# Second block of a fused two-block kernel: k_dil's projection before the first turns, a first quarter of w_out before the last turns, and the last columns by halves of the tokens

## The chip, the cores and the metric

One core of one Trainium2 chip runs the whole program. The metric is device time in microseconds (us) of one launch. Before: median 1310.07 us of three runs (1309.26 to 1310.48).

## The reference, cut to what matters

The first block (a mixer and an expert-choice mixture of 16 experts) is not touched. The second block works on x of 256 tokens x 1024 columns, all in fp32:

```python
h = rms_norm_2(x, mix_norm_g[i])
u = h @ w_in[i]                       # 1024 -> 4096
dq, dk, dv, bq, bk, bv, z = jnp.split(u, IN_SPLIT_IDX, axis=-1)
# dq, dk, bq, bk are normalised over heads of 64
a = diff_attention(dq, dk, dv, lam, diff_slopes)   # 4 heads, two softmaxes each
a = rms_norm_2(a, diff_sub_norm_g[i]) * (1.0 - lam_init)
b = dilated_attention(bq, bk, bv, dil_slopes)      # 8 heads
y = jnp.concatenate([a, b], axis=-1) * jax.nn.silu(z)
x = x + y @ w_out[i]
gate = jax.nn.sigmoid(rms_norm_2(x, ple_norm_g[i]) @ w_ple_gate[i])
x = x + gate * (p[i] @ w_ple_proj[i])
```

## The kernel before, in words

**Weights.** A large product is done as three fp32r matmuls: weights and activations are each split into a high part and a remainder (`split_product`). `split(name, i)` is the work for one 1 MB slot of weights: ScalarE copies it to fp32r (the high part, L1458), then VectorE subtracts (the low part, L1849); TensorE waits for the latter. There are three places for high parts, so ScalarE can start a slot's copy only when TensorE has done the third slot before it.

**Units.** TensorE works through `TAIL_UNITS` in order. A unit is a projection (`q_diff`, `k_diff`, `q_dil`, `k_dil`, `v_diff`, `v_dil`: `rows_product`, 48 matmuls of 512 columns; `z0`, `z1`: 96 of 256) or a set of 8 transposes of 128x128 (the `turn_` units) or a product of weights of the attention with v (`pv_`). Unit u writes banks 0 and 1 of PSUM if u is even, 2 and 3 if odd, so it needs those that unit u-2 filled to have been read (`begin`, semaphores `tfree`). Of most units ScalarE reads the first bank and VectorE the second; both banks of q_diff, k_diff, q_dil and k_dil are read by ScalarE alone (a Square and a Copy each, L1675 and L1676).

**Scores.** After the units in `SCORES_AFTER`, `score_product(a)` (L1300, 16 matmuls) fills banks 4 to 7: a = 0, 1 are the two halves of the queries of the differential attention, 2, 3 those of the dilated. It waits for the reads of turn_q and turn_k. VectorE then does `score_rows(a)` (L2262, four ops) and `score_max(a)` (L2267), ScalarE `exponentials(a)` (L1655, eight ops), VectorE for a = 0, 1 `diff_weights(a)` (L2273 to L2279), and `turn_w0` and `turn_w1` transpose what comes out. `qk_sums` (L2230, L2232), `head_root` (ScalarE, L1661) and `qk_rows` (L2239, L2243) normalise the heads of one projection; a turn_q or turn_k unit waits for its qk_rows.

**Order.** Each engine's order of work is written out by hand, with waits on semaphores between engines. Nothing overtakes on VectorE or ScalarE: a unit's read stands in the written order. In the kernel before, on VectorE, score_rows(1) and score_max(1) follow qk_rows(2), and qk_sums(3), diff_weights(0), v_diff's read, qk_rows(3), diff_weights(1), v_dil's read and turn_w0's come behind them; ScalarE has exponentials(1) directly behind the split of v_dil's second slot, ahead of v_diff's read and both splits of z0.

**End.** `out_product(0..3)` multiplies with quarters of w_out into banks 4 to 7, once `cat_rest` has given the gated activations (`yt_ready`). `add_half(n)` (L2366) adds columns half n to x, `turn_quarter` (L883) transposes it by quarters, `split_pair` makes high parts (ScalarE, L1463) and low ones (VectorE, L1859), and four `columns_rows` products with w_gate follow.

Of the kernel before, what the change touches and what calls it, by code (L numbers as in the profile page):

```python
# [24 lines left out]
P = 128  # L25
SEQ, D = 256, 1024
TT = SEQ // P
KD = D // P
# [32 lines left out]
def shape_constants():  # L61
# [11 lines left out]
    for window, dilation in ((128, 1), (512, 4), (2048, 16)):  # L73
# [16 lines left out]

OPENING = ("fourier_in", "v0", "c0")
STEPS, STEP_K = 4, 2
TAIL_UNITS = [("q_diff", 2), ("k_diff", 2), ("q_dil", 2), ("turn_k_diff", 0), ("turn_q_diff", 0), ("scale_row", 0), ("k_dil", 2),
              ("v_diff", 2), ("v_dil", 2), ("turn_w0", 0), ("turn_k_dil", 0), ("turn_q_dil", 0), ("turn_w1", 0), ("pv_diff", 0),
              ("z0", 2), ("turn_e0a", 0), ("turn_e0b", 0), ("pv_dil0", 0), ("z1", 2), ("turn_e1a", 0), ("turn_e1b", 0),
              ("turn_cat0", 0), ("pv_dil1", 0), ("turn_cat1", 0)]

SCORES_AFTER = {"scale_row": 0, "k_dil": 1, "turn_w1": 2, "turn_e0b": 3}

ROWS_UNITS = ("fourier_in", "q_diff", "k_diff", "v_diff", "q_dil", "k_dil", "v_dil")  # L100

# [16 lines left out]
def build(nc, t, out):  # L118
    ctx = ExitStack()
    with ctx:  # L120
# [613 lines left out]
        def _(pe):  # L734
# [115 lines left out]
                        before_last(last)  # L850
                last.then_inc(slot_used, 1)

            def rows_product(s, u, await_pair=None):

                for i in range(2):
                    w = split_slot(s + i, k=FG, n=BANK)
                    for pair in range(2) if await_pair else (None,):
                        if await_pair:
                            await_pair(2 * i + pair)
                        for tt in range(TT):  # L860
                            for kk in (2 * pair, 2 * pair + 1) if await_pair else range(FG):
                                k = FG * i + kk
                                last = split_product(bank(2 * (u % 2) + tt), [a[:, k, tt * P:(tt + 1) * P] for a in (ht_hi, ht_lo)],
                                                     [h[:, kk, :] for h in w], k == 0, k == KD - 1)
                            if k == KD - 1 and tt == 0:
                                end_first(last)
                        if await_pair and i and pair == 0:
                            turn_stream_back()
                    last.then_inc(slot_used, 1)

            def begin(sems, u):

                for j in range(2):
                    if reads_before(sems, u):
                        pe.wait_ge(sems[pair_of(sems, u) + j], reads_before(sems, u))

            def turn_quarter(rows, q, b):

                for c in range(2):
                    for tt in range(TT):  # L880
                        to = bank(b, c=2, t=TT, m=P)[:, c, tt, :]
                        cols = slice((2 * q + c) * P, (2 * q + c + 1) * P)
                        last = nc.tensor.transpose(to, rows[:, tt, cols], ident)  # L883
                last.then_inc(norm_turned, 1)

            def sum_partitions(b):
# [417 lines left out]
            def out_product(i):  # L1304

                pe.wait_ge(yt_ready, i + 1)
                w = split_slot(first_slot["w_out"] + i, k=2, n=D)
                for n in range(2):
                    for kk in range(2):
                        k = 2 * i + kk  # L1310
                        for tt in range(TT):
                            last = split_product(bank(4 + 2 * tt + n), [a[:, k, tt * P:(tt + 1) * P] for a in (ht_hi, ht_lo)],
                                                 [h[:, kk, n * BANK:(n + 1) * BANK] for h in w], k == 0, k == KD - 1)
                    if i == 3 and n == 0:
                        last.then_inc(out_half, 1)
                last.then_inc(slot_used, 1)

            for u, (name, slots) in enumerate(TAIL_UNITS):
                begin(tfree, u)
                if name == "scale_row":  # L1320
                    pe.wait_ge(xr_ready, 4)
                    for tt in range(TT):
# [2 lines left out]
                elif name in ("z0", "z1"):  # L1325
                    transposed_product(first_slot[name], u, (ht_hi, ht_lo))
                elif name in IN2_CHUNK:
                    rows_product(first_slot[name], u, await_entry if u == 0 else None)
                elif name.startswith(("turn_q", "turn_k")):
                    i = ("turn_q_diff", "turn_k_diff", "turn_q_dil", "turn_k_dil").index(name)  # L1330
                    pe.wait_ge(qn_ready, 2 * i + 2)
                    for j in range(2):
                        for c in range(2):
                            for tt in range(TT):
                                last = nc.tensor.transpose(bank(2 * (u % 2) + j, c=2, t=TT, m=P)[:, c, tt, :],  # L1335
                                                           qn[i][:, tt, (2 * j + c) * P:(2 * j + c + 1) * P], ident)
                        end_first(last) if j == 0 else end_second(last, 0)
                elif name.startswith("turn_w"):

                    a = int(name[6])  # L1340
                    pe.wait_ge(w_ready, a + 1)
                    for j in range(2):
                        for c in range(2):
                            for kk in range(TT):
                                last = nc.tensor.transpose(bank(2 * (u % 2) + j, c=2, t=TT, m=P)[:, c, kk, :],
                                                           scores[a][:, 2 * (2 * j + c), kk * P:(kk + 1) * P], ident)
                        end_first(last) if j == 0 else end_second(last, 0)
                elif name.startswith("turn_e"):
                    a, part = int(name[6]), "ab".index(name[7])
                    pe.wait_ge(exps_done, 3 + a)  # L1350
                    for j in range(2):
                        for c in range(2):
                            for kk in range(TT):
                                last = nc.tensor.transpose(bank(2 * (u % 2) + j, c=2, t=TT, m=P)[:, c, kk, :],
                                                           scores[a][:, 4 * part + 2 * j + c, kk * P:(kk + 1) * P], ident)
                        end_first(last) if j == 0 else end_second(last, 0)
# [19 lines left out]
                else:  # L1376
# [3 lines left out]
                    else:  # L1380
                        await_read(pe, tfree, tail_u["pv_dil0"])
                        await_read(pe, tfree, tail_u["pv_dil1"])
                    for j in range(2):
                        for c in range(2):
                            for tt in range(TT):
                                last = nc.tensor.transpose(bank(2 * (u % 2) + j, c=2, t=TT, m=P)[:, c, tt, :],
                                                           cat[:, tt, (4 * i + 2 * j + c) * P:(4 * i + 2 * j + c + 1) * P], ident)
                        end_first(last) if j == 0 else end_second(last, 0)
                if name in SCORES_AFTER:
                    score_product(SCORES_AFTER[name])  # L1390
            pe.wait_ge(scores_read, 16)
            for i in range(4):
                out_product(i)
            await_read(pe, tfree, len(TAIL_UNITS) - 2)
            await_read(pe, tfree, len(TAIL_UNITS) - 1)
            def await_half(q):

                if q % 2 == 0:
                    pe.wait_ge(x_ready, X_MIXED + 6 + q)

            for q in range(4):
                await_half(q)
                turn_quarter(x, q, q)
            pe.wait_ge(x_ready, X_MIXED + 8)
            for c in range(4):
                columns_rows(first_slot["w_gate"] + c, lambda tt: bank(gate_bank(c, tt))[:, 0:HALF], (ht_hi, ht_lo),
# [5 lines left out]
        def _(act):  # L1412
# [331 lines left out]
            split("k_dil", 0)  # L1744
            split("k_dil", 1)
            unit("q_dil")
            unit("turn_k_diff")
            unit("turn_q_diff")
            split("v_diff", 0)
            unit("scale_row")  # L1750
            head_root(2)
            split("v_diff", 1)
            exponentials(0)
            split("v_dil", 0)
            unit("k_dil")
            split("v_dil", 1)
            exponentials(1)
            head_root(3)
            unit("v_diff")
            split("z0", 0)  # L1760
            split("z0", 1)
            unit("v_dil")
            unit("turn_w0")
# [45 lines left out]
        def _(dve):  # L1809
# [552 lines left out]
            def add_half(n):  # L2362

                cols = slice(n * BANK, (n + 1) * BANK)
                for tt in range(TT):
                    V.tensor_tensor(x[:, tt, cols], x[:, tt, cols], bank(4 + 2 * tt + n), ALU.add).then_inc(x_ready, 1)  # L2366

            split_entry(0)
# [30 lines left out]
            split("k_dil", 0)  # L2399
            split("k_dil", 1)  # L2400
            scale_x()
            unit("turn_k_diff")
            qk_sums(2)
            unit("turn_q_diff")
            score_rows(0)
            split("v_diff", 0)
            unit("scale_row")
            score_max(0)
            split("v_diff", 1)
            qk_rows(2)  # L2410
            split("v_dil", 0)
            score_rows(1)
            score_max(1)
            split("v_dil", 1)
            qk_sums(3)
            lambda_sums()
            diff_weights(0)
            unit("v_diff")
            qk_rows(3)
            diff_weights(1)  # L2420
            unit("v_dil")
            unit("turn_w0")
# [23 lines left out]
            unit("turn_e1a")  # L2446
            unit("turn_e1b")
            cat_gate(0)
            split("w_out", 1)
            dil_rows(1)  # L2450
            cat_rest(0, 0)
            cat_rest(0, 1)
            z_gate(1)
            cat_gate(1)
# [2 lines left out]
            split("w_out", 3)  # L2457
            cat_rest(1, 1)
            split("w_gate", 0)
            dve.wait_ge(out_half, 1)  # L2460
            add_half(0)
            dve.wait_ge(slot_used, first_slot["w_out"] + 4)
            add_half(1)
            for q in range(4):
                split_pair(q, q, col[:, C_PLE:C_PLE + KD], 4)
# [52 lines left out]
```

## Time and profile before

| What | Value |
|---|---|
| median of three runs | 1310.07 us |
| profiled execution: its time, its span | 1309.2 us, 1307.4 us |
| TensorE busy, over the span | 978.1 us (75%) |
| VectorE, ScalarE busy | 385.5 us (29%), 247.1 us (19%) |
| mean granted TensorE clock, share of full speed | 0.882 |
| projections of the second block begin | 1130.99 us |
| last VectorE op ends | 1305.14 us |

Times in views are from the start of the span. In a timeline a row is start, duration, engine, line, operation, operands and count; the brackets behind it give how long the engine had been idle and what ended that. A row's duration includes a tail of some 0.1 us in which the engine's next instruction may already start, so the pitch between the starts of neighbouring rows is what work costs in a queue. In the chain of work that ended last, matmuls stand without this overlap.

### The profile page before, as it was taken

The page shows a single profiled execution, that of the slowest core. Times are in us where ns is not written, and L with a number is a line of the kernel's source. Part 1 is how long each engine was busy: PE and PEld are TensorE (multiplying, and loading weights), DVE is VectorE, ACT ScalarE, POOL GpSimd, SP SyncE. Part 2 cuts the span into 40 slices and gives each one's busy share as a digit, 9 for nine tenths or more (in the row PEclk, how much of TensorE's full clock was granted, in tenths as well). Part 3 has the DMA queues.
Part 4 walks back from the last instruction along what each step waited for, and adds up shares of the span by engine and source line. Part 5 has one row for each costly group of instructions (what it writes and reads, how often), then busy time and mean ns, then how long its engine had stood idle before and what let it go on. Part 6 is the DMA issues. An engine that isn't in the chain of part 4 may idle for free.

```text
span 1307.4 us, 15592 instructions
## 1 busy us (share of the span) xinstructions
PE 978.1 (75%) x6744; PEld 559.2 (43%) x6744; DVE 385.5 (29%) x590; ACT 247.1 (19%) x376; POOL 21.3 (2%) x47
## 2 busy tenths in 40 slices
PE   9999999968565665646666656666665675899998
PEld 7899998323121221212122121212121221478988
DVE  5888866200010110000011000001010000488865
ACT  4454434000000000000000000000000000467744
POOL 2000200000000000000000000000000000000000
PEclk9999999999778878788778787879788878999999
DMA  9998999999999999999999999999999999965230
GB/s 337 389 386 326 314 384 420 401 429 431 426 430 433 432 431 432 425 432 437 428 430 431 429 430 438 431 428 430 431 430 435 431 433 418 397 226 164 95 129 33
DMA packets 70204, 496.43 MB, mean 380 GB/s; under 512 B 4842, under 2 KB 27002, under 8 KB 49680
## 3 DMA queue, kind: packets, MB, share of 16 engines
q1 hardware_dynamic: 67840, 489.11, 90.6%
q0 software_dynamic: 2080, 6.55, 1.6%
q8 instruction: 35, 0.57, 0.2%
q10 hardware_dynamic: 240, 0.11, 0.0%
q14 instruction: 9, 0.07, 0.0%
HBM read 494.71 MB, written 1.06 MB: 379 GB/s over the span
## 4 chain that ended last, share of the span: by engine, by line
DMA 56%; PE 39%; SPq 2%; DVE 1%; issue 1%; ACT 0%; DVEq 0%
DMA ring<-in_w_down_e 23%; DMA ring<-in_w_up_e 18%; DMA ring<-in_w_gate_e 15%; PE psum L748 8%; PE psum L750 8%; PE psum L749 8%; PE psum L1217 7%; PE psum L1247 4%; SPq L571 1%; PE psum L1258 1%; SPq L584 1%; DMA ring<-in_w_in 1%; PE psum L1300 1%; PE psum L1194 1%; PE psum L1335 0%
## 5 line engine op out<-in xcount | busy, mean ns | idle before, releaser
L1217 PE MATMUL psum<-ring,arena 128*32 128x512 f32 x2048 | 300.4, 734 | 186.1 <-DMA ring<-in_w_up_e 109.8
L1247 PE MATMUL psum<-ring,arena 128*32 128x512 f32 x976 | 158.8, 777 | 104.6 <-DMA ring<-in_w_down_e 103.9
L1217 PEld LDWEIGHTS psum<-ring,arena 128*32 128x32 f32 x2048 | 69.4, 129 | 377.5 <-issue 168.5
L1247 PEld LDWEIGHTS psum<-ring,arena 128*32 128x32 f32 x976 | 41.5, 132 | 205.2 <-issue 136.9
L1849 DVE TENSOR_TENSOR ring_r<-ring,ring_r 128x2048 fp32r<-128x2048 f32 x49 | 111.1, 2288 | 35.8 <-ACT ring_r L1458 35.6
L1626 ACT ACTIVATE arena<-psum 128x512 f32<-128x512 f32 x16 | 9.6, 598 | 532.1 <-PE psum L1217 532.1
L748 PE MATMUL psum<-ht_hi,ring_r 128*128 128x256 f32 x384 | 108.5, 283 | 0.0
L750 PE MATMUL psum<-ht_hi,ring_r 128*128 128x256 f32 x384 | 107.3, 279 | 0.0
L749 PE MATMUL psum<-ht_lo,ring_r 128*128 128x256 f32 x384 | 107.2, 279 | 0.0
L2211 DVE TENSOR_TENSOR arena<-psum,arena 128x512 f32<-128x512 f32 x32 | 20.6, 686 | 291.8 <-PE psum L1247 291.8
L1458 ACT ACTIVATE ring_r<-ring 128x2048 fp32r<-128x2048 f32 x49 | 92.5, 1910 | 29.7 <-PE psum L750 22.6
L2204 DVE TENSOR_TENSOR arena<-psum,arena 128x512 f32<-128x512 f32 x16 | 11.1, 692 | 266.9 <-ACT arena L1626 266.9
L748 PE MATMUL psum<-ring_r,ht_hi 128*128 128x256 f32 (+1 forms) x256 | 87.0, 340 | 0.2 <-issue 0.2
L750 PE MATMUL psum<-ring_r,ht_lo 128*128 128x256 f32 (+1 forms) x256 | 86.9, 339 | 0.0
L749 PE MATMUL psum<-ring_r,ht_hi 128*128 128x256 f32 (+1 forms) x256 | 86.1, 336 | 0.0
L1258 PE MATMUL psum<-arena 128*128 128x256 f32 x256 | 65.8, 415 | 13.5 <-DVE arena L2211 13.5
L748 PEld LDWEIGHTS psum<-ht_hi,ring_r 128*128 128x128 f32 x384 | 72.1, 188 | 1.6 <-issue 1.4
L749 PEld LDWEIGHTS psum<-ht_lo,ring_r 128*128 128x128 f32 x384 | 72.2, 188 | 0.2
L750 PEld LDWEIGHTS psum<-ht_hi,ring_r 128*128 128x128 f32 x384 | 72.1, 188 | 0.0
L1258 PEld LDWEIGHTS psum<-arena 128*128 128x128 f32 x256 | 51.8, 208 | 39.7 <-DVE arena L2211 32.1
L1630 ACT ACTIVATE arena<-psum 128x512 f32<-128x512 f32 x16 | 9.6, 597 | 294.6 <-PE psum L1235 294.6
L748 PEld LDWEIGHTS psum<-ring_r,ht_hi 128*128 128x128 f32 x256 | 48.1, 188 | 6.3 <-issue 1.1
(307 smaller groups left out, 934.1 us busy)
## 6 DMA issues: line engine op xcount, KB each, us to landing
ring<-in_w_gate_e SPq DMA_DIRECT2D x23, 4096.0 KB, 33.3
ring<-in_w_up_e SPq DMA_DIRECT2D x22, 4096.0 KB, 33.3
ring<-in_w_down_e SPq DMA_DIRECT2D x21, 4096.0 KB, 33.9
ring<-in_w_up_e SPq DMA_DIRECT2D x16, 2048.0 KB, 36.3
ring<-in_w_in SPq DMA_DIRECT2D x31, 1024.0 KB, 9.9
ring<-in_w_gate_e SPq DMA_DIRECT2D x14, 2048.0 KB, 36.5
ring<-in_w_down_e SPq DMA_DIRECT2D x14, 2048.0 KB, 36.9
ring<-in_w_ada SPq DMA_DIRECT2D x16, 1024.0 KB, 9.8
```

The source lines that it names most:

```text
L571: sp.dma_start(slot_in(s, k=FG, part=2, n=STEP_K * P)[:, :, part, :], head_stream[s][:, :, part, :]).then_inc(loaded[place(s)], 16)
L584: sp.dma_start(slot_in(s, k=FG, n=BANK)[:, rows, :], head_stream[s][:, rows, :]).then_inc(opening_loaded[name], 16)
L748: mm(to, left[0], right[0], start=start, stop=False)
L749: mm(to, left[0], right[1], start=False, stop=False)
L750: return mm(to, left[1], right[0], start=False, stop=stop)
L1194: last = mm(bank(tt), pt[k][:, tt * P:(tt + 1) * P], w_pp[:, k, n * BANK:(n + 1) * BANK], start=(k == 0), stop=(k == 1))
L1217: last = mm(psum[32 * g:32 * g + 32, b, :].rearrange("s (q c) -> s q c", c=4), cur[h][:, k, :], w[:, g // 2, :, g % 2 * 4:g % 2 * 4 + 4], ...
L1247: last = mm(psum[32 * q:32 * q + 32, 2 + n, :], act_t[:, f % 4, (f // 4) * CAP:(f // 4 + 1) * CAP], w[:, kk, n * BANK:(n + 1) * BANK], sta ...
L1258: last = mm(bank(4 + q, c=2, s=SEQ)[:, c, :], y[:, n, at:at + P], gwt.rearrange("p t m -> p (t m)"), start=False, stop=True, skip_group_ch ...
L1458: f(ring_r[part_place[s]][:], ring[:, place(s), :], ACT.Copy).then_inc(hi_ready, 1)
L1849: V.tensor_tensor(ring_r[place(s)][:], ring[:, place(s), :], ring_r[part_place[s]][:].bitcast(F32), ALU.subtract).then_inc(lo_ready, 1)
L2211: V.tensor_tensor(y[:, n, :], bank(2 + n), gf_row[:, n * BANK:(n + 1) * BANK], ALU.mult).then_inc(y_ready, 1)
```

## The change

TensorE: unit k_dil moves ahead of turn_k_diff, turn_q_diff and scale_row (which changes the pair of banks of these four), and the second scores follow v_diff and not k_dil. The wait for the second bank of a projection or a turn stands behind the work into the first bank. out_product(0) is done between pv_dil1 and turn_cat1. In the last w_out quarter the second half of the columns is done token half by token half, and the addition and the turns behind it follow by token halves. VectorE and ScalarE get new orders in the first part; VectorE does cat_rest(0, 0) before the split of w_out's second quarter. The slots of weights are loaded in the same order as before. The core of the diff (the second-bank wait is added in the same way in the other turn branches):

```diff
-TAIL_UNITS = [("q_diff", 2), ("k_diff", 2), ("q_dil", 2), ("turn_k_diff", 0), ("turn_q_diff", 0), ("scale_row", 0), ("k_dil", 2),
+TAIL_UNITS = [("q_diff", 2), ("k_diff", 2), ("q_dil", 2), ("k_dil", 2), ("turn_k_diff", 0), ("turn_q_diff", 0), ("scale_row", 0),
               ("v_diff", 2), ("v_dil", 2), ("turn_w0", 0), ("turn_k_dil", 0), ("turn_q_dil", 0), ("turn_w1", 0), ("pv_diff", 0),
...
-SCORES_AFTER = {"scale_row": 0, "k_dil": 1, "turn_w1": 2, "turn_e0b": 3}
+SCORES_AFTER = {"scale_row": 0, "v_diff": 1, "turn_w1": 2, "turn_e0b": 3}
...
@@ rows_product @@
                         for tt in range(TT):
+                            if i == 0 and tt and not await_pair and sems is not None:
+                                begin(sems, u, (1,))
...
-            def begin(sems, u):
-
-                for j in range(2):
+            def begin(sems, u, banks=(0, 1)):
+
+                for j in banks:
...
-            def turn_quarter(rows, q, b):
-
-                for c in range(2):
-                    for tt in range(TT):
-                        to = bank(b, c=2, t=TT, m=P)[:, c, tt, :]
+            def turn_quarter(rows, q, b, await_rows=None):
+
+                for c, tt in [(c, tt) for tt in range(TT) for c in range(2)] if await_rows else [(c, tt) for c in range(2) for tt in range(TT)]:
+                    if await_rows and c == 0:
+                        await_rows(tt)
...
@@ out_product @@
                 for n in range(2):
-                    for kk in range(2):
+                    rows_last = i == 3 and n == 1
+                    for kk, tt in [(kk, tt) for tt in range(TT) for kk in range(2)] if rows_last else [(kk, tt) for kk in range(2) for tt in range(TT)]:
...
+                        if rows_last and k == KD - 1 and tt == 0:
+                            last.then_inc(out_half, 1)
...
             for u, (name, slots) in enumerate(TAIL_UNITS):
-                begin(tfree, u)
+                by_bank = name.startswith("turn_") or (name in ROWS_UNITS and u > 0)
+                begin(tfree, u, (0,) if by_bank else (0, 1))
...
                     for j in range(2):
+                        if j:
+                            begin(tfree, u, (1,))
...
-            pe.wait_ge(scores_read, 16)
-            for i in range(4):
+                if name == "pv_dil1":
+                    pe.wait_ge(scores_read, 16)
+                    out_product(0)
+            for i in range(1, 4):
                 out_product(i)
...
@@ ScalarE @@
             unit("q_dil")
+            head_root(2)
+            split("v_diff", 0)
+            split("v_diff", 1)
+            unit("k_dil")
             unit("turn_k_diff")
             unit("turn_q_diff")
-            split("v_diff", 0)
             unit("scale_row")
-            head_root(2)
-            split("v_diff", 1)
+            split("v_dil", 0)
+            head_root(3)
             exponentials(0)
-            split("v_dil", 0)
-            unit("k_dil")
             split("v_dil", 1)
-            exponentials(1)
-            head_root(3)
             unit("v_diff")
             split("z0", 0)
+            exponentials(1)
             split("z0", 1)
             unit("v_dil")
             unit("turn_w0")
@@ VectorE: add_half @@
                 for tt in range(TT):
+                    if n == 0:
+                        dve.wait_ge(out_half, 1)
+                    elif tt == 0:
+                        dve.wait_ge(out_half, 2)
+                    else:
+                        dve.wait_ge(slot_used, first_slot["w_out"] + 4)
...
@@ VectorE: order @@
             scale_x()
+            qk_sums(2)
+            split("v_diff", 0)
+            qk_rows(2)
+            split("v_diff", 1)
             unit("turn_k_diff")
-            qk_sums(2)
             unit("turn_q_diff")
+            unit("scale_row")
             score_rows(0)
-            split("v_diff", 0)
-            unit("scale_row")
             score_max(0)
-            split("v_diff", 1)
-            qk_rows(2)
+            qk_sums(3)
             split("v_dil", 0)
+            lambda_sums()
+            qk_rows(3)
+            split("v_dil", 1)
+            diff_weights(0)
+            unit("v_diff")
             score_rows(1)
             score_max(1)
-            split("v_dil", 1)
-            qk_sums(3)
-            lambda_sums()
-            diff_weights(0)
-            unit("v_diff")
-            qk_rows(3)
             diff_weights(1)
             unit("v_dil")
             unit("turn_w0")
...
             cat_gate(0)
+            cat_rest(0, 0)
             split("w_out", 1)
             dil_rows(1)
-            cat_rest(0, 0)
             cat_rest(0, 1)
```

## Rows read from the trace of the kernel before

**Rows 1.** Busy time by engine from 1130 to 1308 us, with clock and DMA.

```profile
1130.00:1308.00 178.00, 171.02 (x1067) 149.69 (x1065) 133.71 (x186) 113.96 (x193) 0.70 (x1) 1.00 0.43 149
```

**Rows 2.** All waits of TensorE from 1160 to 1308 us.

```profile
PE psum L1300 <- issue: 1.0, 1, 1.0
PE psum L1386 <- DVE arena L2359: 0.7, 1, 0.7
PE psum L1335 <- issue: 0.5, 1, 0.5
PE psum L883 <- DVE arena L2366: 0.5, 1, 0.5
```

**Rows 3.** Chain that ended last: turn_k_diff, scores 0 and 1, turn_w0, scores 2.

```profile
1166.37 0.87 PE psum L1335 x8
...
1170.25 2.00 PE psum L1300 x16
...
1183.53 1.93 PE psum L1300 x16
...
1207.84 0.87 PE psum L1345 x8
...
1211.75 1.93 PE psum L1300 x16
```

**Rows 4.** Timeline of VectorE: scores, softmax and splits, then two late operations.

```profile
1171.50 2.49 DVE L2262 SCALAR_TENSOR_TENSOR arena<-psum,ring 128x512 f32<-128x512 f32 x4 [1.35 <-PE psum L1300]
...
1191.91 2.29 DVE L2267 TENSOR_REDUCE arena<-arena 128x8 f32<-128x2048 f32 x1
1194.12 2.28 DVE L1849 TENSOR_TENSOR ring_r<-ring,ring_r 128x2048 fp32r<-128x2048 f32 x1
1196.31 1.27 DVE L2230 TENSOR_REDUCE arena<-arena 128x8 f32<-128x512 f32 x2
1197.62 0.18 DVE L2232 TENSOR_SCALAR arena<-arena 128x16 f32<-128x16 f32 x1
...
1198.08 0.20 DVE L2273 RECIPROCAL arena<-arena 128x8 f32<-128x8 f32 x1
...
1201.35 0.74 DVE L2342 TENSOR_SCALAR ring<-psum,arena 128x512 f32<-128x512 f32 x1
1202.02 0.24 DVE L2239 RECIPROCAL arena<-arena 128x16 f32<-128x16 f32 x1
...
1203.50 0.20 DVE L2273 RECIPROCAL arena<-arena 128x8 f32<-128x8 f32 x1
...
1254.13 0.76 DVE L2359 TENSOR_TENSOR arena<-psum,arena 128x256 f32<-128x256 f32 x2
...
1279.64 3.26 DVE L1859 SCALAR_TENSOR_TENSOR ht_lo<-psum,arena,ht_hi 128x256 fp32r<-128x256 f32 x8
```

**Rows 5.** Timeline of ScalarE: exponentials of both score halves, splits, last high parts.

```profile
1185.26 1.90 ACT L1458 ACTIVATE ring_r<-ring 128x2048 fp32r<-128x2048 f32 x1
...
1194.23 0.51 ACT L1655 ACTIVATE arena<-arena 128x256 f32<-128x256 f32 x1 [1.02 <-DVE arena L2267]
...
1198.31 1.28 ACT L1661 ACT_TABLE_LOAD   x1
1199.60 0.22 ACT L1661 ACTIVATE arena<-arena 128x16 f32<-128x16 f32 x1
...
1278.77 3.17 ACT L1463 ACTIVATE ht_hi<-psum,arena 128x256 fp32r<-128x256 f32 x8 [2.49 <-PE psum L883]
```

**Rows 6.** Timeline of TensorE in the expert stage: work behind two idle stretches.

```profile
724.00 6.46 PE L1217 MATMUL psum<-ring,arena 128*32 128x512 f32 x32 [3.30 <-DMA ring<-in_w_gate_e]
...
1085.48 4.92 PE L1217 MATMUL psum<-ring,arena 128*32 128x512 f32 x32 [6.18 <-DMA ring<-in_w_gate_e]
```

**Rows 7.** Busy time and granted clock (third number from the right) behind them.

```profile
724.00:729.00 5.00, 5.00 (x24) 1.36 (x28) 0.00 (x0) 0.00 (x0) 0.00 (x0) 0.50 0.97 419
...
1085.00:1088.00 3.00, 2.52 (x12) 0.60 (x16) 0.00 (x0) 0.00 (x0) 0.00 (x0) 0.50 0.99 426
```

More of the change, by code:

```diff
@@ L851, in columns_rows, with rows_product @@
                 last.then_inc(slot_used, 1)
-            def rows_product(s, u, await_pair=None):
+            def rows_product(s, u, await_pair=None, sems=None):
                 for i in range(2):
@@ L869, in rows_product @@
                     last.then_inc(slot_used, 1)
-            def begin(sems, u):
-                for j in range(2):
+            def begin(sems, u, banks=(0, 1)):
+                for j in banks:
                     if reads_before(sems, u):
                         pe.wait_ge(sems[pair_of(sems, u) + j], reads_before(sems, u))
-            def turn_quarter(rows, q, b):
-                for c in range(2):
-                    for tt in range(TT):
-                        to = bank(b, c=2, t=TT, m=P)[:, c, tt, :]
-                        cols = slice((2 * q + c) * P, (2 * q + c + 1) * P)
-                        last = nc.tensor.transpose(to, rows[:, tt, cols], ident)
+            def turn_quarter(rows, q, b, await_rows=None):
+                for c, tt in [(c, tt) for tt in range(TT) for c in range(2)] if await_rows else [(c, tt) for c in range(2) for tt in range(TT)]:
+                    if await_rows and c == 0:
+                        await_rows(tt)
+                    to = bank(b, c=2, t=TT, m=P)[:, c, tt, :]
+                    cols = slice((2 * q + c) * P, (2 * q + c + 1) * P)
+                    last = nc.tensor.transpose(to, rows[:, tt, cols], ident)
                 last.then_inc(norm_turned, 1)
@@ L1308, in out_product @@
                 for n in range(2):
-                    for kk in range(2):
+                    rows_last = i == 3 and n == 1
+                    for kk, tt in [(kk, tt) for tt in range(TT) for kk in range(2)] if rows_last else [(kk, tt) for kk in range(2) for tt in range(TT)]:
                         k = 2 * i + kk
-                        for tt in range(TT):
-                            last = split_product(bank(4 + 2 * tt + n), [a[:, k, tt * P:(tt + 1) * P] for a in (ht_hi, ht_lo)],
-                                                 [h[:, kk, n * BANK:(n + 1) * BANK] for h in w], k == 0, k == KD - 1)
+                        last = split_product(bank(4 + 2 * tt + n), [a[:, k, tt * P:(tt + 1) * P] for a in (ht_hi, ht_lo)],
+                                             [h[:, kk, n * BANK:(n + 1) * BANK] for h in w], k == 0, k == KD - 1)
+                        if rows_last and k == KD - 1 and tt == 0:
+                            last.then_inc(out_half, 1)
                     if i == 3 and n == 0:
@@ L1327, in _ @@
                 elif name in IN2_CHUNK:
-                    rows_product(first_slot[name], u, await_entry if u == 0 else None)
+                    rows_product(first_slot[name], u, await_entry if u == 0 else None, tfree)
                 elif name.startswith(("turn_q", "turn_k")):
@@ L1342, in _ @@
                     for j in range(2):
+                        if j:
+                            begin(tfree, u, (1,))
                         for c in range(2):
@@ L1351, in _ @@
                     for j in range(2):
+                        if j:
+                            begin(tfree, u, (1,))
                         for c in range(2):
@@ L1383, in _ @@
                     for j in range(2):
+                        if j:
+                            begin(tfree, u, (1,))
                         for c in range(2):
@@ L1395, in _ @@
             await_read(pe, tfree, len(TAIL_UNITS) - 1)
-            def await_half(q):
-                if q % 2 == 0:
-                    pe.wait_ge(x_ready, X_MIXED + 6 + q)
             for q in range(4):
-                await_half(q)
-                turn_quarter(x, q, q)
+                turn_quarter(x, q, q, (lambda tt: pe.wait_ge(x_ready, X_MIXED + 4 + q + tt + 1)) if q % 2 == 0 else None)
             pe.wait_ge(x_ready, X_MIXED + 8)
@@ L2459, in _ @@
             split("w_gate", 0)
-            dve.wait_ge(out_half, 1)
             add_half(0)
-            dve.wait_ge(slot_used, first_slot["w_out"] + 4)
             add_half(1)
```

## The prediction

> **What bounds the kernel now.** I read the busy time and clock of the second block first, then TensorE's waits, the chain of work that ended last, and the timelines of VectorE and ScalarE. In the first view [rows 1] TensorE is busy for 171.0 of 178 us at full clock, and DMA is at 0.43. So the second block runs at TensorE's pace. The waits [rows 2] are what a new order can win: four waits of 1.0, 0.7, 0.5 and 0.5 us, 2.7 us in all. More than that no edit here can give, since no matmul is taken out. The reader is to see that this ceiling is 0.2% of the kernel, and that a measurement of this kernel tells no less than 0.2% (2.6 us) from no change. The other view to keep in mind is the timeline of VectorE [rows 4], 133.7 us busy of 178 in [rows 1]: it isn't the bound, but it is close to one, and its work is in a fixed order.
>
> **Part 1: k_dil ahead of the turns.** Before, TensorE waited 0.5 us ahead of turn_q_diff, because ScalarE had yet to read q_dil's second bank, and 1.0 us ahead of scores 0, because VectorE did qk_sums(2) before its read of turn_q_diff [rows 2]. The new order puts k_dil (48 matmuls) behind q_dil. One projection costs (1207.84 - 1185.46) / 2 = 11.19 us: two of them lie between the end of scores 1 (1183.53 + 1.93) and turn_w0 [rows 3]. So:
> - q_dil ends at 1166.37, k_dil at 1177.56, turn_k_diff (0.87) at 1178.43.
> - turn_q_diff now shares banks with k_dil, whose last bank ScalarE has read 1.40 us after its end (before: turn_k_diff from 1166.37 for 0.87, then the wait of 0.53, L1335 [rows 2, 3]). Only its second half waits: 1178.96, and ends at 1179.4.
> - VectorE reads it at once: 0.74 for such an op [rows 4] and 0.1 on either side for the hand-over. Scores 0 start at 1180.3 and end at 1182.3.
> - v_diff ends at 1193.5, scores 1 at 1195.4, v_dil at 1206.6, turn_w0 at 1207.5.
>
> Before, v_dil ended at 1207.84. So 1.2 us of the 1.5 are won up to here. The weights come no later: the places of k_dil's slots come free 5.9 us earlier, and the queue of loads has its order unchanged.
>
> **Part 2: what the late scores do to VectorE.** Scores 0 move from 1170.25 to 1180.3, 10 us later, while turn_w1, which needs the end of the whole softmax of scores 1, stays where it was. Between them VectorE has to do, in the written order, with pitches from [rows 4]:
> - score_rows(0) starts 1.25 us behind the scores (1171.50 against 1170.25): 1181.55, 2.49 long; score_max(0) 2.21 (1191.91 to 1194.12): 1186.25.
> - qk_sums(3) and lambda together 1.77 (1196.31 to 1198.08), the split of v_dil's first slot 2.19 (1194.12 to 1196.31), qk_rows(3) 1.48 (1202.02 to 1203.50): 1191.7.
> - Then it idles. ScalarE gets the means at 1187.7 (1.49 behind the start of qk_sums), does a root (0.22), a load of the table (1.28), eight exponentials (4.08, 1194.23 to 1198.31) and the split of v_dil's second slot (1.90) [rows 5]: 1195.2.
> - split 2.19, diff_weights(0) 3.27 (1198.08 to 1201.35), v_diff's read 0.67, score_rows(1) 2.49, score_max(1) 2.29: 1206.1.
> - ScalarE's exponentials(1) 4.08: 1210.2. diff_weights(1) 3.27: 1213.5.
>
> Behind diff_weights(1) on VectorE stand the reads of v_dil's second bank and of turn_w0's. On ScalarE the split of z0's second slot and the reads of v_dil's and turn_w0's first banks stand behind exponentials(1). turn_k_dil needs v_dil's banks. VectorE's read ends at 1214.2, so TensorE, which is out of work at 1207.5, gets at most half of turn_k_dil done in between and goes on at 1214.3. What is left up to scores 2 is half a turn and two turns. A turn costs 0.98 with its boundary ((1211.75 - 1207.84) / 4) against 0.87 alone [rows 3]. 1214.3 + 0.45 + 1.96 = 1216.7. Scores 2 began at 1211.75 before: **+4.9 us**, in which the 1.2 us won are already counted. From scores 2 on all orders are those of before until pv_dil1, and TensorE had no wait there that could take this up [rows 2], so the 4.9 us stay.
>
> **Part 3: the clock.** This wait of 6.8 us, broken only by half a turn, is longer than any in this part of the kernel, which ran at full clock [rows 1]. In the expert stage TensorE waited 3.30 and 6.18 us for weights [rows 6]; behind either wait the granted clock was 0.50, the lower level (1.2 GHz): for the whole of 724 to 729, and for 2.52 us of work up to 1088 [rows 7]. Half a clock loses half of that time: 2.5 and 1.3 us. The second wait is the nearer one in length; I take **+1.4 us**, with 0 (the half turn keeps the clock up) and 2.5 as ends.
>
> The Trainium skill (TensorE: Matmul & The Clock Gate, section on Part 1, the HAM clock gate) says that an idle array is put to half its clock and gets the full clock back only after it has been kept busy for some time. The trace agrees, with 0.50 behind both waits. By that rule the time would be 1315.8 us; without it, 1314.4. It speaks against this change: a wait of this size costs more than its length.
>
> **Part 4: first quarter of w_out ahead of turn_cat1.** Before, turn_cat1 waited 0.7 us for VectorE's reads of pv_dil1 (L2359) [rows 2, 4]. Now 24 matmuls (24 x 11.19 / 48 = 5.6 us) stand in between and hide the reads. They need cat_rest(0, 0), which now precedes the split of w_out's second slot (2.2 us) and so comes about as much earlier: before, it started behind L2359's end at 1254.89; now it is there by some 1253.7, and pv_dil1 ends at 1254.3 (0.7 before turn_cat1, which starts 0.1 behind L2359's end). **-0.7 us**, with 0 if cat_rest is late. Splits and cat_rest(1, 0) keep some 2 us ahead of the next quarters.
>
> **Part 5: last columns by token halves.** The 0.5 us wait of the last turns (L883) goes. But the next product needs low parts from VectorE (L1859, 8 ops in 3.26 us from 1279.64) [rows 4], and these need ScalarE's high parts, which start at 1278.77 behind the first turned quarter and take 0.40 each: the first pair is there at 1279.6 [rows 5]. The edit moves neither. VectorE's eight ops pace TensorE here, so the wait moves behind the turns. **-0.1 us**, between 0 and -0.5.
>
> **Part 6: second-bank waits** in the middle of 17 units. A wait that is fulfilled shows no cost, at worst the 0.11 of a boundary: 0 to 1.9 us. **+0.2 us**, near the former: the projections' matmuls run on across a unit's start, waits and all.
>
> **Sum**: 4.9 + 1.4 - 0.7 - 0.1 + 0.2 = +5.7 us. The profiled execution took 1309.2 us, 0.9 below the median, so the sum in it is 1314.9; on the median it is **1315.8 us** (+0.4%).
>
> **Rivals.**
> - *The clock stays up* (0.18): the wait is there, but the half turn in it is enough. +4.3: 1314.4. For it: the idle stretch is cut into about 5.1 and 1.2 us. Against it: 3.30 us were enough before [rows 6, 7].
> - *The change does what it says* (0.08), the case of the other side: VectorE and ScalarE are through with v_dil's reads in time. It decides when v_dil's second bank is read by 1208.4, when turn_w0 ends; it needs 5.8 us off a chain of ops whose durations are all known, for instance if exponentials(1) didn't lie in it (4.1) and ScalarE's stretch ahead of v_dil's split (3.5) neither. Then 1.2 + 0.7 + 0.1 are won: 1308.1 us. With all four waits gone, -2.7: 1307.4, just at the bound of what can be told.
> - *A shorter wait* (0.12): the chain is 2 to 4 us shorter than summed, since hand-overs or the idle 3.5 us of VectorE are less. The clock doesn't fall, and 0 to 2.5 us are lost: 1310 to 1312.6.
> - *The likeliest* (0.62): wait and clock, 1315.8; own range 1314.4 to 1318.
>
> **Range and chances.** The known terms with the ends of the unknown give +3.7 (4.9 - 0.7 - 0.5) to +9.3 (4.9 + 2.5 + 1.9). All ends at once on the high side is unlikely, so I stop at 1318.2; below I go to 1312.4, into the shorter wait. Slower by over 0.2%: 0.62 + 0.18 and a part of the shorter wait, 0.84. Within 0.2%: the rest of it and most of the case that works, 0.12. Faster: 0.04.
>
> **What would show it.** After the change: no wait of TensorE before scores 0 above 0.4 us; scores 0 near 1180.3; diff_weights(1) ending near 1213.5; a wait of 5 us or more at L1335 behind turn_w0, ended by VectorE or ScalarE; a granted clock under 1 in the few us from 1210 on; scores 2 5 to 6.5 us later than 1211.75; no wait at L1386; a wait in the first w_gate product in place of that at L883. I am wrong if VectorE's ops between scores 0 and v_dil's read take much under 32 us, or if TensorE gets v_dil's banks from an engine that I have placed wrongly in the order.

## The result and the profile after

Changed kernel: median 1316.61 us of five runs (1314.57 to 1316.84), beside 1310.48 us for the kernel before on the same chip (five runs, 1309.26 to 1311.43). Ratio 1.0047, 95% interval 1.0036 to 1.0058: slower by 6.1 us, or 0.5%. The profiled execution took 1316.68 us, with a span of 1314.9.

In that profile the second block starts at 1132.00 us, against 1130.99 before (the table above). c1 below shows that this 1.0 us isn't the change's. Where times of the two are compared, 1.0 is taken off those of after.

The waits of TensorE from 1155 to 1310 us in the changed kernel, which answer to [rows 2] (line: total, number, longest):

```profile
PE psum L1343 <- ACT ring L1698: 5.0, 1, 5.0
PE psum L748 <- DVE ht_lo L1869: 0.6, 1, 0.6
PE psum L1343 <- DVE ring L2352: 0.6, 1, 0.6
PE psum L1303 <- issue: 0.3, 1, 0.3
```

L1343 are the turns (sets of 8 transposes) of q and k, L1698 and L2352 the reads of a v unit's banks on ScalarE and VectorE, L1303 the scores, L748 the first w_gate product. The old waits at the turns and at pv_dil1 are gone, that at the scores has shrunk to 0.3, and 5.0 + 0.6 us are new, behind turn_w0. The chain that ended last shows what is in them; it leaves TensorE at scores 0 and comes back to it only at 1215.37 (some rows left out):

```profile
1181.37 1.15 PE psum L1303 x8
1182.61 2.50 DVE arena L2272 x4
1185.13 2.29 DVE arena L2277
...
1189.08 1.28 ACT L1665
1190.38 1.14 ACT arena L1665 x5
...
1194.43 1.81 ACT ring_r L1468
1196.26 2.29 DVE ring_r L1859
...
1201.81 0.66 DVE ring L2352
1202.48 2.40 DVE arena L2272 x4
1204.90 2.30 DVE arena L2277
1207.22 1.13 ACT arena L1665 x5
...
1212.98 1.67 DVE arena L2289 x4
1214.65 0.67 DVE ring L2352
1215.37 2.82 PE psum L1343 x12
1218.19 1.71 PE psum L1355 x8
1219.90 2.21 PE psum L1303 x16
1222.11 3.77 PE psum L1375 x32
```

In [rows 3] the stretch from 1183.53 to 1211.75 was TensorE's own. Now each link is an op of VectorE or ScalarE that waited for the one above: rows and maximum of scores 0, the table and eight exponentials, v_dil's second split, rows and maximum of scores 1, exponentials, diff_weights(1), v_dil's read. Two things hang on the last link: the read of v_dil (1214.65), for which turn_k_dil waits, and the clock. Busy time and granted clock (third number from the right) of the changed kernel around the wait:

```profile
1209.00:1212.00 3.00, 0.00 (x0) 0.00 (x0) 0.63 (x3) 3.00 (x11) 0.00 (x0) 1.00 0.86 340
1212.00:1214.00 2.00, 0.31 (x2) 0.31 (x3) 1.97 (x7) 2.00 (x3) 0.00 (x0) 0.90 0.04 14
1214.00:1220.00 6.00, 5.44 (x26) 4.71 (x26) 3.48 (x7) 2.41 (x5) 0.00 (x0) 0.50 0.00 0
1220.00:1221.00 1.00, 1.00 (x8) 0.86 (x10) 1.00 (x2) 1.00 (x1) 0.00 (x0) 0.78 0.00 0
```

TensorE idles at full clock, and about when it has work again (1213.69) the clock falls to 0.50, the lower level of 1.2 GHz, and stays there for six more us. [Rows 7] showed the same level behind the waits of the expert stage.

### The profile page after: what moved, and what is told of

It is laid out like the page before. It is cut to its first block, busy times and chain, and to the rows that moved or that the text cites. A ratio compares the mean times of both kernels' runs of the same rounds, so it can differ in the third digit from the quotient of the medians.

```text
span 1314.9 us, 15589 instructions
## 1 busy us (share of the span) xinstructions
PE 979.9 (75%) x6744; PEld 560.7 (43%) x6744; DVE 385.8 (29%) x590; ACT 244.3 (19%) x374; POOL 21.7 (2%) x47
## 4 chain that ended last, share of the span: by engine, by line
DMA 56%; PE 38%; DVE 2%; SPq 2%; ACT 1%; issue 1%; DVEq 0%
DMA ring<-in_w_down_e 23%; DMA ring<-in_w_up_e 17%; DMA ring<-in_w_gate_e 15%; PE psum L748 7%; PE psum L749 7%; PE psum L750 7%; PE psum L1220 7%; PE psum L1250 4%; SPq L571 1%; PE psum L1261 1%; DMA ring<-in_w_in 1%; SPq L584 1%; ACT arena L1665 1%; PE psum L1385 1%; PE psum L1197 1%
## 5 line engine op out<-in xcount | busy, mean ns | idle before, releaser
L748 PE MATMUL psum<-ht_hi,ring_r 128*128 128x256 f32 x384 | 109.8, 286 | 0.0
L748 PE MATMUL psum<-ring_r,ht_hi 128*128 128x256 f32 (+1 forms) x256 | 87.1, 340 | 0.8 <-DVE ht_lo L1869 0.6
L748 PEld LDWEIGHTS psum<-ht_hi,ring_r 128*128 128x128 f32 x384 | 72.3, 188 | 1.7 <-issue 1.4
L1261 PE MATMUL psum<-arena 128*128 128x256 f32 x256 | 61.8, 396 | 13.6 <-DVE arena L2221 13.6
L1261 PEld LDWEIGHTS psum<-arena 128*128 128x128 f32 x256 | 48.9, 196 | 36.9 <-DVE arena L2221 30.5
L748 PEld LDWEIGHTS psum<-ring_r,ht_hi 128*128 128x128 f32 x256 | 48.1, 188 | 7.0 <-issue 1.9
```

Source lines behind the costliest of these rows:

```text
L748: mm(to, left[0], right[0], start=start, stop=False)
L1261: last = mm(bank(4 + q, c=2, s=SEQ)[:, c, :], y[:, n, at:at + P], gwt.rearrange("p t m -> p (t m)"), start=False, stop=True, skip_group_ch ...
```

## The experiments

All are timed over five rounds beside the kernel before on the same chip, but for c1.

**e1: the late parts alone.** Units, scores and both orders of the first part as before; the early w_out quarter, token halves and second-bank waits kept.

```diff
-TAIL_UNITS = [("q_diff", 2), ("k_diff", 2), ("q_dil", 2), ("k_dil", 2), ("turn_k_diff", 0), ("turn_q_diff", 0), ("scale_row", 0),
+TAIL_UNITS = [("q_diff", 2), ("k_diff", 2), ("q_dil", 2), ("turn_k_diff", 0), ("turn_q_diff", 0), ("scale_row", 0), ("k_dil", 2),
-SCORES_AFTER = {"scale_row": 0, "v_diff": 1, "turn_w1": 2, "turn_e0b": 3}
+SCORES_AFTER = {"scale_row": 0, "k_dil": 1, "turn_w1": 2, "turn_e0b": 3}
...
```

> The first part as in the kernel before (units, scores and the orders of VectorE and ScalarE), with the early first quarter of w_out, the token halves and the second-bank waits kept. Theory (the loss is all in the wait behind turn_w0): no wait at L1343 over 0.6 us, the wait for pv_dil1's reads gone, 0.8 us less than before, so about 1309.7 us. Rival (the waits in the middle of the units cost TensorE, up to 1.9 us, or the early quarter disturbs VectorE): as before or slower, 1310.5 to 1312 us.

Measured: 1308.9 us against 1310.13, ratio 0.9989 (0.998 to 0.9998). No wait at L1343 is left, 1.2 us are waited at the scores (the 1.0 of before, since VectorE still does qk_sums(2) between its reads). So the late parts and the waits in the middle of units win a little over a microsecond, 0.4 us more than expected, and have no part in the loss.

**e2: the first part alone.** out_product(0) behind turn_cat1 again, cat_rest(0, 0) behind dil_rows(1), no token halves.

```diff
-                if name == "pv_dil1":
-                    pe.wait_ge(scores_read, 16)
-                    out_product(0)
-            for i in range(1, 4):
+            pe.wait_ge(scores_read, 16)
+            for i in range(4):
...
```

> The changed kernel with its end as before: out_product(0) behind turn_cat1, cat_rest(0, 0) behind the reads of pv_dil1, no token halves. Theory (the late parts win 0.7 to 0.9 us and have no part in the loss): 1317.4 us, with a wait of 0.7 us at turn_cat1 back. Rival (the late parts lose something behind a late first part): at or below the changed kernel's 1316.6.

Measured: 1317.41 us against 1310.7, ratio 1.0055 (1.0042 to 1.0069). The profile has the 5.0 + 0.6 us at L1341 (the turns) and again 0.7 and 0.5 at turn_cat1 and the last turns. The difference to the changed kernel, 0.8 us, is in the expected direction, but the two intervals overlap; the profiles carry the reading. From the second block's first product to VectorE's last op it is 180.96 us in e2 (1131.35 to 1312.31) and 180.19 in the changed kernel (1132.00 to 1312.19), again 0.8 us. This stretch leaves out the scatter of what comes before it; in two profiles of one kernel it agrees to 0.2 us (c1).

**e3: reads ahead of the softmax.** v_dil's, turn_w0's and turn_k_dil's banks are read ahead of diff_weights(1) on VectorE, v_dil's ahead of exponentials(1) on ScalarE.

```diff
@@ ScalarE @@
-            exponentials(1)
-            split("z0", 1)
             unit("v_dil")
+            exponentials(1)
             unit("turn_w0")
             unit("turn_k_dil")
+            split("z0", 1)
@@ VectorE @@
-            diff_weights(1)
             unit("v_dil")
             unit("turn_w0")
             unit("turn_k_dil")
+            diff_weights(1)
```

> The changed kernel, but VectorE reads v_dil's, turn_w0's and turn_k_dil's banks ahead of diff_weights(1), and ScalarE reads v_dil's ahead of exponentials(1) and turn_w0's and turn_k_dil's right behind them. Theory (a good part of the wait is reads queued behind the softmax): the 5.0 us wait splits into about 2 us ahead of turn_q_dil and 2 us ahead of turn_w1, TensorE does two turns in between, scores 2 start near 1215.6 instead of 1219.9, and the time is 1312 to 1314 us. Rival (only the dependency of turn_w1 on diff_weights(1) counts): turn_w1 cannot start before 1214.6 in either order and gives back at most what two turns take, 1.8 us at full clock: 1314.8 us or more.

Measured: 1314.66 us against 1310.13, ratio 1.0032 (1.002 to 1.0044), just above my range for the theory and at the edge of the rival's. TensorE's timeline in e3 from turn_k_dil to pv_diff:

```profile
1212.03 1.09 PE L1343 MATMUL psum<-arena 128*128 128x128 f32 x8 [2.20 <-ACT arena L1713]
1215.02 1.94 PE L1355 MATMUL psum<-arena 128*128 128x128 f32 x8 [1.90 <-DVE arena L2289]
1216.89 3.47 PE L1303 MATMUL psum<-ring 64*128 64x256 f32 x16
```

The wait splits as expected, into 2.2 and 1.9 us; but the clock still falls (0.50 from 1214 to 1219), so the scores take 3.47 us where at full clock they take 2.00 [rows 3], and start at 1216.9 instead of 1219.9, later than the 1215.6 expected. Both theories were half right: 3 us of the delay of scores 2 are reads in a queue, and the dependency of turn_w1 on diff_weights(1) keeps the rest.

**e4: the softmax first.** v_dil's second split ahead of exponentials(0), score_rows(1) and score_max(1) ahead of diff_weights(0).

```diff
@@ ScalarE @@
-            exponentials(0)
             split("v_dil", 1)
+            exponentials(0)
@@ VectorE @@
             split("v_dil", 1)
-            diff_weights(0)
-            unit("v_diff")
             score_rows(1)
             score_max(1)
+            diff_weights(0)
+            unit("v_diff")
             diff_weights(1)
```

> The changed kernel, but ScalarE splits v_dil's second slot ahead of exponentials(0), and VectorE does score_rows(1) and score_max(1) ahead of diff_weights(0) and v_diff's read. Theory (the order of VectorE and ScalarE makes the wait, not the place of k_dil and the scores): diff_weights(1) ends near 1208 instead of 1214.6, no wait over 0.6 us between turn_w0 and scores 2, clock at 1.00 throughout, and the edits win what they were summed to win, 2.0 us: 1308.5 us. Rival (scores 10 us later can't be caught up by any order): a wait of 3 us or more at turn_w1 and 1313 us or more.

Measured: 1307.44 us against 1310.13, ratio 0.9979 (0.997 to 0.9988). That beats both kernels. VectorE's timeline in e4:

```profile
1196.06 2.48 DVE L2272 SCALAR_TENSOR_TENSOR arena<-psum,ring 128x512 f32<-128x512 f32 x4 [0.75 <-PE psum L1303]
1198.58 2.29 DVE L2277 TENSOR_REDUCE arena<-arena 128x8 f32<-128x2048 f32 x1
...
1206.66 1.67 DVE L2289 SCALAR_TENSOR_TENSOR arena<-arena 128x256 f32<-128x256 f32 x4
1208.25 0.74 DVE L2352 TENSOR_SCALAR ring<-psum,arena 128x512 f32<-128x512 f32 x1
```

score_rows(1) starts right behind the second scores (it waits 0.75 us for TensorE), diff_weights(1) ends at 1208.3, and v_dil's bank is read 0.2 us after TensorE has filled it. Chain rows of e4:

```profile
1208.09 0.87 PE psum L1355 x8
1208.96 1.75 PE psum L1343 x16
1210.71 0.87 PE psum L1355 x8
1211.60 2.00 PE psum L1303 x16
```

No wait is left there, and the clock stays at 1.00. The place of k_dil and the late scores cost nothing once VectorE and ScalarE have their softmax first. They even give something: from the first product to VectorE's last op e4 takes 171.28 us and e1, without the new first part, 172.25.

**e8: only VectorE's order mended.** As e4, with ScalarE's order as in the changed kernel.

```diff
@@ VectorE @@
-            diff_weights(0)
-            unit("v_diff")
             score_rows(1)
             score_max(1)
+            diff_weights(0)
+            unit("v_diff")
```

> The changed kernel, but VectorE does score_rows(1) and score_max(1) ahead of diff_weights(0) and v_diff's read; ScalarE's order is kept, with v_dil's second split behind exponentials(0). Theory (the chain scores 0 to v_dil's read, summed op by op): score_max(1) ends at 1203.3 instead of 1207.2, diff_weights(1) at 1210.8 instead of 1214.6, so a wait of about 3 us behind turn_w0 is left, 4 us less than before with its clock: 1311 to 1312.5 us. Rival (the order of these two on VectorE was the whole cause): no wait, 1307.5 us as with both orders mended.

Measured: 1310.67 us against 1310.7, ratio 1.0001 (0.9992 to 1.001), the time of the kernel before and 0.3 us below my range. The waits behind turn_w0 in e8:

```profile
PE psum L1343 <- ACT ring L1698: 1.1, 1, 1.1
PE psum L1343 <- DVE ring L2352: 1.0, 1, 1.0
```

2.1 us are left instead of 5.6, so 3.5 us came from VectorE's order, and the clock did not fall (1.00 in every stretch). The rival is out: with VectorE's order mended alone there is still a wait, and what is left of it goes in e4, which differs only in ScalarE's split ahead of exponentials(0). ScalarE's order mended alone was not run, so how much that edit would give without the other isn't shown.

**e5 and e5b: TensorE kept busy.** Matmuls into bank 4, whose results nobody reads, behind turn_w0; 40 of them, then 22.

```diff
+                if name == "turn_w0":
+                    pe.wait_ge(scores_read, 8)
+                    for _ in range(40):
+                        mm(psum[:, 4, 0:P], ones, ident, start=True, stop=True)
```

> The changed kernel with 40 matmuls of 128 columns into bank 4 behind turn_w0, which nobody reads, so that TensorE isn't idle in the wait. Theory (the fall of the clock is part of the loss): the granted clock stays at 1.00, what follows the wait (turns, scores 2) takes about 4.3 us up to pv_diff instead of 6.7, and the time is 2.4 us under the changed kernel's, 1314.2 us. Rival (the clock costs nothing beside the wait, since the turns wait for VectorE and ScalarE anyway): within 0.5 us of the changed kernel's 1316.6.

Measured: 1316.94 us against 1310.13, ratio 1.005 (1.0036 to 1.0064). By the time alone the rival had won. The chain of e5 shows why that reading would be wrong:

```profile
1209.15 8.93 PE psum L1406 x80
1218.09 1.75 PE psum L1343 x16
1219.83 0.87 PE psum L1355 x8
```

The 40 matmuls are 80 in the trace and take 8.93 us, 0.11 each. The filling held TensorE up to 1218.09, 2.4 us past the end of VectorE's read of v_dil in the same profile (1214.98 + 0.74). What follows takes 4.63 us up to pv_diff, at full clock. The experiment was mis-sized, and was repeated with 22.

> The changed kernel with 22 instead of 40 matmuls of 128 columns behind turn_w0. In the run with 40 the clock stayed at 1.00, but each matmul went through the array twice (80 rows, 8.9 us), so that the filling itself outlasted the wait by 2.7 us; 22 take 4.9 us and end before VectorE frees v_dil's second bank at 1215.4. Theory (the clock is part of the loss): clock 1.00, from there to pv_diff some 4.2 us instead of 6.7, and 2.5 us less than the changed kernel: 1314.1 us. Rival (the turns wait for VectorE and ScalarE anyway): 1316 us or more.

Measured: 1313.81 us against 1310.7, ratio 1.0028 (1.0017 to 1.0038). The chain of e5b behind v_dil's read:

```profile
1214.84 1.53 PE psum L1343 x12
1216.37 0.87 PE psum L1355 x8
1217.26 2.00 PE psum L1303 x16
1219.26 3.77 PE psum L1375 x32
```

The same twelve and eight transposes and scores take 4.42 us up to pv_diff, against 6.74 in the changed kernel (1215.37 to 1222.11). With the chain of VectorE and ScalarE as it is, the clock alone costs 2.3 us by the chains; by the medians it is 2.8, by the ratios (1.0047 against 1.0028) 2.5, and by the stretch from the first product to VectorE's last op also 2.5 (180.19 against 177.67). The granted clock is 1.00 throughout in e5b, so the clock's part is shown.

**e7: no waits in the middle of a unit.** e4 with both banks awaited at the start.

```diff
-                by_bank = name.startswith("turn_") or (name in ROWS_UNITS and u > 0)
+                by_bank = False
...
-                        if j:
-                            begin(tfree, u, (1,))
```

> As the kernel with the softmax first (1307.4 us), but every unit waits for both of its banks at its start again. Theory: only turn_q_diff gains by the later wait, since its second bank is k_dil's; it waits some 0.5 us more, and the others as before: 1307.9 us. Rival (fulfilled waits in the middle of a unit cost up to 0.11 us each): 1306 us.

Measured: 1309.31 us against 1310.7, ratio 0.9986 (0.9977 to 0.9995). That is 0.9 us by the ratios above e4, though the two intervals overlap, and more than the 0.5 expected. By the stretch from the first product to VectorE's last op it is 1.2 us (172.47 us in e7, 171.28 in e4). The theory's part is there: TensorE waits 0.5 us ahead of turn_q_diff's transposes, and from the first product to scores 0 e7 takes 0.4 us more. The other 0.8 us lie behind turn_w0. In e7 the turns of turn_k_dil and turn_q_dil and the scores behind them stand so in the chain:

```profile
1207.79 0.87 PE psum L1349 x8
1208.81 1.94 PE psum L1339 x16
1210.76 1.06 PE psum L1349 x8
1211.83 1.93 PE psum L1301 x16
```

From turn_w0 to scores 2 it is 4.04 us in e7 and 3.51 in e4: waits in the middle win 0.5 us here, and 0.3 more at the turns of the dilated weights (1.9 against 1.75 us for sixteen transposes, twice). Neither theory named that: a unit's second bank is free a little later than its first, and waiting for it at the start holds back the first half. In e7 turn_k_dil starts at 1208.81, 0.1 us behind the end of VectorE's read of v_dil (1207.96 + 0.75), and turn_w1 at 1210.76, 0.1 us behind the end of its read of turn_k_dil (1209.91 + 0.75).

**e6: no token halves.** e4 with the last columns as in the kernel before.

```diff
-                        if rows_last and k == KD - 1 and tt == 0:
-                            last.then_inc(out_half, 1)
...
-                    elif tt == 0:
-                        dve.wait_ge(out_half, 2)
```

> As the kernel with the softmax first (0.9979 of the kernel before), but the last quarter of w_out, the addition and the last turns not by token halves. Theory (VectorE's low parts pace TensorE there, so the token halves only move a wait): a wait of 0.5 us back at the last turns, less of one in the first w_gate product, and at most 0.1 to 0.2 us more, which the times can't tell. Rival (the whole wait of 0.5 us was won by the halves): 0.5 us more, and the first w_gate product starting 0.5 us later against the end of the last w_out product.

Measured: 1308.18 us against 1310.44, ratio 0.9983 (0.9974 to 0.9992); the interval takes in e4's 0.9979. The chain at the end of the last w_out product, first e6, then e4:

```profile
1277.30 1.30 DVE arena L2378 x2
1278.64 1.09 PE psum L886 x8
1279.73 0.25 PE psum L748
```

```profile
1277.10 0.45 PE psum L886 x4
1277.58 0.85 ACT ht_hi L1473 x2
1278.45 0.89 DVE ht_lo L1869 x2
...
1279.47 0.36 PE psum L748
```

From the end of the product to the first w_gate matmul it is 2.43 us without the halves and 2.37 with them, so the token halves win next to nothing. The wait has moved from the turns (0.5) to the low parts (0.6), as summed.

**c1: the kernel before once more**, for a second profile.

> The kernel before once more, for a second profile. The profiled execution of before has the second block's first product 1.0 us earlier in its span than the profile of the changed kernel, and 1.0 to 1.4 us earlier than those of the experiments. Theory (this is the scatter of the expert stage, which no edit touches): the first product at 1131.5 to 1133.5 us here. Rival (the changed code delays what comes ahead of it): again at 1131.0.

Measured: one time, 1311.4 us. The second block's first product starts at 1133.06 us, 2.1 us later than in the first profile of the same kernel, and the four waits are the same to the tenth. From there to VectorE's last op it is 173.88 us, against 173.73 in the first profile. So the start of the second block scatters by 2 us between executions of one kernel, while its own length agrees to 0.2 us in these two, and the 1.0 us between the profiles of before and after says nothing of the change.

## Why the prediction was right

1316.6 us were measured, 1315.8 predicted; the range, the direction and the cause hold. One term was under-sized (part 3), and one had the wrong sign (part 6); they err in opposite directions, so that the sum came this near is in part luck.

- *Part 1.* Scores 0 were put at 1180.3 and start at 1180.4 (1181.37 - 1.0); the 0.3 us wait ahead of them was seen coming (under 0.4). turn_w0 starts at 1206.9 (1207.87 - 1.0), 1.0 us earlier than before instead of 1.2.
- *Part 2.* diff_weights(1) was to end at 1213.5; v_dil's read starts behind it at 1214.65 - 1.0 = 1213.65. All the ops in between lie within 0.2 us of the sum. e4 and e8 show that this chain is the cause, and that it is one of order: with the same units and scores the whole loss goes.
- *Part 3* was under-sized. The clock fell, as the likeliest case had it, but cost 2.3 to 2.8 us instead of 1.4. I took the expert stage's 2.52 us at half clock, the wait nearest in length. Here it was six us and more at 0.50, nearer the other row, 724 to 729. The rival in which the clock stays up is out for this kernel; with 2.1 us of waiting in e8 it did happen.
- *Part 4.* 0.7 us, shown by the wait's absence and by its return in e2, where parts 4 and 5 together are worth the 0.8 us of the sum.
- *Part 5.* -0.1 as summed: 2.43 against 2.37 us (e6, e4).
- *Part 6* failed: I priced the waits in the middle at +0.2 us with 0 as the best end, and they win. The step that failed is "a wait that is fulfilled shows no cost, at worst the 0.11 of a boundary". The 0.11 a turn in [rows 3] was no boundary's cost but a wait for the second bank, which the change takes away. The kernel before shows it, on TensorE and on VectorE:

```profile
1208.73 1.94 PE L1335 MATMUL psum<-arena 128*128 128x128 f32 x16
1210.68 1.07 PE L1345 MATMUL psum<-arena 128*128 128x128 f32 x8
```

```profile
1207.88 0.75 DVE L2342 TENSOR_SCALAR ring<-psum,arena 128x512 f32<-128x512 f32 x1 [1.02 <-PE psum L750]
1209.83 0.75 DVE L2339 TENSOR_SCALAR ring<-psum,arena 128x512 f32<-128x512 f32 x1 [0.39 <-PE psum L1335]
```

turn_k_dil (1208.73) starts 0.1 us behind the end of VectorE's read of v_dil (1208.63), and turn_w1 (1210.68) 0.1 us behind the end of its read of turn_k_dil (1210.58). In e1, with the waits in the middle, the same stretch from turn_w0 to scores 2 takes 3.51 us instead of 3.91. e7 against e4 gives 1.2 us in all, but the 0.4 at turn_q_diff were already in part 1 ("only its second half waits"), so 0.8 us are part 6's own with the softmax first. In the changed kernel, where the long wait covers the turns behind turn_w0, it is the 0.3 at the turns of the dilated weights.

The measured sum, by chains: pv_diff starts 7.4 us later than in [rows 3] (1222.11 - 1.0 against 1211.75 + 1.93). Of these 2.3 are the clock's (1.4 in the sum), and 5.1 parts 1 and 2 (4.9 in the sum). Behind it 1.0 us is won back (0.6 in the sum, with parts 4 to 6), and 6.4 are left against 5.7; by the medians it is 6.1.

The case in which the change does what it says became real with two edits of order (e4): 2.7 us won by the medians, 2.5 by the stretch from the first product, against the 2.0 that it was priced at. That also corrects the ceiling of 2.7 us which the prediction read from [rows 2]. e4 still waits 0.6 and 0.3 us and yet wins 2.5, so a part of what it wins isn't in the list: waits of 0.2 us and less, such as those at the turns above, stand in no row of it.

## What to carry to other kernels

When work is moved ahead on the engine that sets the pace, sum the chain that starts at what has now become late, on the other engines and in their written order, up to the next thing that the first engine needs; here it is 33 us of ops and waits (1181.37 to 1214.65) against 27 us of TensorE's work. All that TensorE's listed waits could give was 2.7 us, while one late softmax cost 5 and the clock half as much again. The remedy is an order of that chain by who is waited for: two swaps turned +0.5% into -0.2%.

Wait for a bank where it is first written and not at the head of the unit. And before a filling is used to test the clock, its own length has to be read from the trace: the first one here misled by being too long.

## What the runs showed of the hardware

- After an idle stretch of 5.0 us, four transposes and 0.6 us more of idling, the clock was at 0.50 for over six us, though TensorE was busy for 5.44 of the 6 us from 1214 to 1220. With waits of 2.2 and 1.9 us and 1.1 us of transposes in between (e3) it also fell; with 1.1 and 1.0 us (e8) it stayed at 1.00. The Trainium skill (TensorE: Matmul & The Clock Gate, section on the HAM clock gate) says that an idle array falls to half its clock; these runs agree.
- An fp32 matmul of 128x128 with 128 columns, outside the fp32r path, shows as two in the trace, 0.11 us each at a granted clock of 1.00 (e5: 40 issued, 80 rows, 8.93 us).
